# Weight splits, dealt gate tiles and the order of the query and key splits in the second attention of a two-block transformer kernel

## The reference

```python
FOX_HEADS = 16
FOX_HEAD_DIM = 64
FOX_SCALE = 1.0 / math.sqrt(FOX_HEAD_DIM)

    proj = u @ w_in[l]
    (cq, ckv, k_pe_raw, z_mla, fq, fk, fv, f_logit, z_fox, gate_a, gate_b) = jnp.split(proj, split_idx, axis=-1)
    ...
    log_f = jax.nn.log_sigmoid((f_logit + fox_forget_b[l]).astype(jnp.float32)).transpose(0, 2, 1)
    cum = jnp.cumsum(log_f, axis=-1)
    o_fox = causal_block_attention(fox_heads(fq), fox_heads(fk), fox_heads(fv), FOX_SCALE, cum)
    o_fox = o_fox.transpose(0, 2, 1, 3).reshape(B, L, FOX_WIDTH)
    y_fox = (o_fox * jax.nn.silu(z_fox)) @ w_br_fox[l]
```

## Time and profile before

| | |
|---|---|
| median of 3 runs | 1583.72 us |
| the runs | 1583.72, 1578.91, 1584.73 us |
| the profiled execution | 1581.14 us |
| its span in the trace | 1579.3 us |
| mean granted TensorE clock | 0.995 of full speed |
| PE busy | 1535.2 us (97%) |
| DVE busy | 837.9 us (53%) |
| ACT busy | 694.3 us (44%) |

### The profile page before, as it was taken

One profiled execution on the slowest core, in us unless ns is written; L12 is line 12 of the kernel. 1 busy time (PEld: TensorE's weight loads), 2 busy tenths in 40 slices (PEclk: granted clock), 3 DMA queues, 4 the chain that ended last, 5 costly groups with the idle time before them and its releaser, 6 DMA issues.

```text
span 1579.3 us, 24007 instructions
## 1 busy us (share of the span) xinstructions
PE 1535.2 (97%) x10287; PEld 1349.9 (85%) x10287; DVE 837.9 (53%) x1234; ACT 694.3 (44%) x1036; POOL 3.6 (0%) x16
## 2 busy tenths in 40 slices
PE   7999999999999999999999899999999999999998
PEld 7999999999999988997888677778899787778888
DVE  6467766644655565653344576643223565543343
ACT  6555666654343222222333655633222766643232
POOL 0000000000000000000000000000000000000000
PEclk9999999999999999999999999999999999999999
DMA  6212112113332232322224100122322111122322
GB/s 228 81 58 84 54 54 72 51 41 135 107 106 82 81 107 81 107 81 97 96 76 125 30 28 1 54 81 85 102 81 81 54 54 54 54 67 81 107 81 81
DMA packets 130541, 125.46 MB, mean 79 GB/s; under 512 B 20169, under 2 KB 128484, under 8 KB 130052
## 3 DMA queue, kind: packets, MB, share of 16 engines
q1 hardware_dynamic: 129956, 120.36, 24.1%
q0 software_dynamic: 464, 3.56, 0.6%
q10 hardware_dynamic: 16, 0.00, 0.0%
HBM read 119.66 MB, written 4.26 MB: 78 GB/s over the span
## 4 chain that ended last, share of the span: by engine, by line
PE 86%; DVE 7%; ACT 4%; issue 3%; DMA 0%; DVEq 0%; SPq 0%; ACTq 0%
PE PS L841 73%; PE PS L953 3%; PE PS L1167 2%; DVE wlo L1786 2%; PE PS L1110 2%; PE PS L1132 2%; DVE small L2303 1%; ACT Pm L1296 1%; ACT xka L1296 1%; ACT whi L1296 0%; PE PS L1115 0%; PE PS L1144 0%; PE PS L1116 0%; PE PS L965 0%; PE PS L1001 0%
## 5 line engine op out<-in xcount | busy, mean ns | idle before, releaser
L841 PE MATMUL PS<-zhi,whi 128*128 128x258 f32 (+2 forms) x1872 | 487.0, 320 | 8.1 <-DVE zlo L1832 3.4
L841 PE MATMUL PS<-zlo,whi 128*128 128x258 f32 (+2 forms) x1872 | 475.4, 314 | 0.0
L841 PE MATMUL PS<-zhi,wlo 128*128 128x258 f32 (+2 forms) x1872 | 474.9, 314 | 0.0
L841 PEld LDWEIGHTS PS<-zhi,whi 128*128 128x128 f32 x1872 | 309.1, 190 | 33.3 <-issue 8.3
L841 PEld LDWEIGHTS PS<-zhi,wlo 128*128 128x128 f32 x1872 | 307.6, 189 | 21.5
L841 PEld LDWEIGHTS PS<-zlo,whi 128*128 128x128 f32 x1872 | 307.9, 189 | 18.8
L1786 DVE TENSOR_TENSOR wlo<-raw,whi 128x2048 fp32r<-128x2048 f32 (+2 forms) x114 | 247.7, 2173 | 123.2 <-ACT whi L1296 122.9
L1296 ACT ACTIVATE whi<-raw 128x2048 fp32r<-128x2048 f32 (+2 forms) x114 | 207.3, 1819 | 155.3 <-DMA raw<-in_w_up 55.9
L1296 ACT ACTIVATE Pm<-PS,small 128x144 f32<-128x144 f32 (+3 forms) x128 | 68.7, 540 | 79.1 <-DVE small L2303 79.1
L2303 DVE TENSOR_REDUCE small<-PS 128x1 f32<-128x144 f32 (+3 forms) x128 | 62.5, 502 | 37.5 <-PE PS L1117 36.8
L841 PE MATMUL PS<-ghi,whi 128*128 128x512 f32 x176 | 69.7, 396 | 2.2 <-DVE glo L2198 2.2
(11 more groups left out here) (351 smaller groups left out, 2157.6 us busy)
## 6 DMA issues: line engine op xcount, KB each, us to landing
raw<-in_w_in SPq DMA_DIRECT2D x50, 1024.0 KB, 5.2
raw<-in_w_up SPq DMA_DIRECT2D x22, 1024.0 KB, 5.1
raw<-in_w_out SPq DMA_DIRECT2D x8, 1024.0 KB, 5.3
raw<-in_w_down SPq DMA_DIRECT2D x8, 1024.0 KB, 5.1
raw<-in_w_br_mla SPq DMA_DIRECT2D x4, 1024.0 KB, 5.4
raw<-in_w_br_fox SPq DMA_DIRECT2D x4, 1024.0 KB, 5.3
raw<-in_w_down SPq DMA_DIRECT2D x4, 768.0 KB, 4.6
hspill<-hT SPq DMA_DIRECT2D x1, 2112.0 KB, 8.7
```

The lines of the kernel that those rows point to most:

```text
L841: ins = mm(o_, l_, r_, start=first, stop=last)
```

## The change

Three edits, all in the second attention.

1. DVE takes the low parts of a weight unit in the same pass in which ACT takes the high part. It no longer stands at the start of pass h+1; it stands at the second block of pass h, behind the reciprocal sums and ahead of the product `omla` and of `split_lo(h+1)` (the new argument `ahead`).
2. The tiles ("xz", 0) and ("xz", 1) are dealt over the passes 13, 14 and 15 in single steps (`XZ_STEPS`); the pass 16 keeps ("xz", 2).
3. ACT makes both copies of the query ahead of both copies of the key. DVE waits for the query's two copies, makes `xqa` and `xqb`, and only then waits for the key's and makes `xkb`. In pass 0 the query is split before the key's tile is taken out of its accumulator.

```diff
+            XZ_STEPS = {(13, 0): ((0, 0),), (13, 1): ((0, 1),), (13, 2): ((0, 2),), (13, 3): ((0, 3),),
+                        (13, 4): ((0, 4), (0, 5)), (14, 0): ((0, 6),), (14, 1): ((0, 7),), (14, 2): ((1, 0),),
...
             def fox_fill(h, i):
+                for x, k in XZ_STEPS.get((h, i), ()):
+                    if k == 0:
+                        portion[0] = gemm_steps(("xz", x))
+                    ins = portion[0](k)
+                    if k == KT - 1:
+                        ins.then_inc(pe_mark, 1)
                 x = h // 2 + 1 + h % 2
                 if x < KT:
                     name = (("xk", "xq")[h % 2], x)
-                elif h - 14 in (0, 1, 2):
-                    name = ("xz", h - 14)
+                elif h == HEADS:
+                    name = ("xz", 2)
...
-                tile_freed(act, ("xk", h // 2))
                 q = fq[h // 2 % 2]
                 A_(xqa[i][r, :], q[r, :], ACT.Copy).then_inc(fox_hi, 1)
+                A_(xqb[i][r, :], q[r, :], ACT.Copy).then_inc(fox_hi, 1)
+                if h == 0:
+                    fk_out(0)
+                tile_freed(act, ("xk", h // 2))
                 A_(xka[i][r, :], fk[r, :], ACT.Copy).then_inc(fox_hi, 1)
-                A_(xqb[i][r, :], q[r, :], ACT.Copy).then_inc(fox_hi, 1)
                 A_(xka[i][o, :], fk[r, :], ACT.Copy).then_inc(fox_hi, 1)
...
-            def attention(A, project, between):
+            def attention(A, project, between, ahead):
...
+                            ahead(h)
                             if h >= 3 and h % 2 == 1:
...
-                dve.wait_ge(fox_hi, 4 * (h + 1))
+                dve.wait_ge(fox_hi, 4 * h + 2)
                 q = fq[h // 2 % 2]
                 V.tensor_tensor(xqa[i][o, :], q[r, :], xqa[i][r, :].bitcast(F32), ALU.subtract).then_inc(fox_lo, 1)
+                V.tensor_copy(xqb[i][o, :], pick[o, h:h + 1].bitcast(F32).broadcast_to([64, SEQ])).then_inc(fox_lo, 1)
+                dve.wait_ge(fox_hi, 4 * h + 4)
                 V.tensor_tensor(xkb[i][r, :], fk[r, :], xka[i][r, :].bitcast(F32), ALU.subtract).then_inc(fox_lo, 1)
-                V.tensor_copy(xqb[i][o, :], pick[o, h:h + 1].bitcast(F32).broadcast_to([64, SEQ])).then_inc(fox_lo, 1)
...
-                w_low(*XU_AT.get(h - 1, ()))
-
-            attention(fox, fox_project, lambda h: split_lo(h + 1) if h < HEADS - 1 else None)
+
+            attention(fox, fox_project, lambda h: split_lo(h + 1) if h < HEADS - 1 else None,
+                      lambda h: w_low(*XU_AT.get(h, ())))
```

More of the change, by code:

```diff
@@ L1728, in fox_project @@
                     act.wait_ge(xv_turned, KT)
-                    fk_out(0)
                     split_hi(0)
@@ L2392, in q_out @@
                                                  in1=trig[:, 0, NM:T], op0=ALU.mult, op1=ALU.mult), n)
-            attention(mla, mla_project, lambda h: None)
+            attention(mla, mla_project, lambda h: None, lambda h: None)
             def gated(kind, A, b):
```

## The result

The changed kernel took 1570.89 us in the median of five runs (1570.11 to 1574.25), the kernel before, beside it, 1581.0 (1578.91 to 1584.73). The ratio is 0.9934, with a 95% interval of 0.9919 to 0.995: 10.1 us less between the medians, 10.4 by the ratio. Run again twice later it gave 0.9924 (0.991 to 0.9938) and 0.9936 (0.9923 to 0.9949). The forecast was 1575.3 with a range from 1571 to 1581.

A forecast was written before the change was run, and what follows sets the result against it. TensorE, busy 97% of the span, was taken to bound the kernel. Terms 1.1 + 1.5 + 0.5 + 1.0 + 3.4 + 1.6 - 0.3 - 0.4 = 8.4 us, off the median 1583.72, gave 1575.3 us, range 1571 to 1581.

The forecast's parts named there:

- the ceiling of this change: Second attention: at most TensorE's 8.8 us of idle time and 1.6 us of slow clock can be won, 10.4 us.
- My terms without clock and groups: Second attention: gains from removed waits, less pass 14's 0.4; left out are clock (1.6) and five more step groups (0.3 lost).
- The estimate of 0.16 us for a break: Dealt gate tiles: by the Trainium skill's formulas each break in TensorE's stream costs 0.16 us, 0.8 us for five.
- passes 4, 8, 12: 0.5 us: Passes 4, 8, 12: maxima of blocks 0 and 1 no longer stand behind the low part; 0.5 us gained.
- Query ahead of key: Passes 0 and 1: DVE starts its splits after two ACT copies, not four; the whole wait goes, 1.1 us.
- Low parts: Moved into DVE's idle time a pass earlier: 1.5 us in passes 2, 6, 10; 0.5 in 4, 8, 12; 1.0 in 1.
- Tiles: Pass 13: dealt gate steps fill all waits, 3.4 us, and save 1.6 of clock; groups cost 0.3, pass 14 waits 0.4.
- Waits that only move on: Rival, passes 1, 4, 8, 12, 14: part of the waits moves on; gain 6.4 us, 1577.3; 23 in 100.
- The clock falls anyway: Rival, thin passes 13 to 15: the clock falls once, 1.6 us come back; gain 6.8, 1576.9; 10 in 100.
- The change does little: Rival: key copies end last, or pass 13's waits reappear in 14 and 15; gain 3.4 or less, 1580.5; 5 in 100.
- The slower case: Rival: low part not covered in eight passes, 18 us added, less 8.4: 10 us slower, 1594; 5 in 100.

The follow-up runs named there:

- e5: The changed kernel with ten stalls of TensorE added on purpose in the five gate tiles behind the attention: 1578.05 us, ratio 0.9966.
- e1: The kernel before with only the third edit, query copies ahead of key copies on ACT and DVE waiting for two, then four: 1575.47 us, ratio 0.9962.
- e2: The kernel before with only the first edit, low parts of the weights taken in the odd pass itself: 1578.46 us, ratio 0.9983.
- e7: The changed kernel with TensorE's first turn ahead of the filling tile in passes 1, 2, 4, 6, 8, 10 and 12: 1569.85 us, ratio 0.9921.
- e9: The changed kernel with TensorE's first turn ahead of the filling tile only in the even passes 2 to 12: 1567.92 us, ratio 0.991.
- e4: The kernel before with the first and third edits, without the dealt tiles: 1575.96 us, ratio 0.9966.
- e3: The kernel before with only the second edit, gate steps dealt six to pass 13 and five each to 14 and 15: 1577.85 us, ratio 0.9979.
- e6: The changed kernel with an unused DVE reduction of some 2.2 us ahead of each low part in the eight odd passes: 1579.47 us, ratio 0.9988.

## Why the prediction was off, point by point

**What bounds the kernel: right, but the ceiling was not one.** TensorE's idle time and its slow clock were what could be won. The sentence "the ceiling of this change is 8.8 + 1.6 = 10.4 us" is wrong: the price of 16 stalls was not in it. With 0.25 each it would have been 14.

**The idle time that goes: right.** My terms without clock and groups, 1.1 + 1.5 + 0.5 + 1.0 + 3.4 - 0.4, make 7.1. In the traces it went from 8.8 in 16 stalls to 1.7 in nine, 7.1. TensorE is busy 7.1 us more of the 210, where I expected some 8.

**The step that failed: each stall was costed at its idle figure.** Seven stalls fewer, at the 0.25 of e5, are 1.75 us that stand in no term. Idle time 7.1, stalls 1.75, clock 1.7 and groups -0.3 make 10.25, against 10.2 measured. Only the sum comes out so well. On top of the idle time, passes 0 and 1 gave 0.55 for one stall fewer, passes 4, 8 and 12 0.2 each, and in pass 13 three stalls fewer and five groups more gave 0.2 together; no run measures the groups alone. The estimate of 0.16 us for a break, which the prediction sets against the dealing, was applied to no stall; e5 measured 0.16 to 0.17 of lost overlap at each. The missing price shows most where stalls are short: "passes 4, 8, 12: 0.5 us" was 1.2. In those the wait itself was right (0.19 each) and its price 0.4 each. e1 and e2 each give that same 0.4 in those passes by different means, and e7 and e9 give 0.39 for each stall of 0.16.

**The second step that failed: the anchor.** I took the sum of one profiled execution off the median of three runs, 1583.72, though that execution itself stood at 1581.14. The five runs beside the changed kernel have a median of 1581.0, the later ones 1581.13 (20), 1581.53 (20) and 1581.74 (9). From 1581.14 the same 8.4 us give 1572.7, inside the range. This was worth 2.6 us, the stalls 1.8. The lower end of the range, 1571, was the ceiling of 10.4 us taken off 1581, so a gain of 10.2 from 1581 ends beside it. With medians of 1569.15, 1570.89 and 1571.33 for the changed kernel it is chance on which side of it one of them falls.

**Query ahead of key: right in mechanism and size** for passes 0 and 1 (2.1 forecast, 2.4 measured). e1 shows it as the strongest of the three alone. DVE's `xqa` waits for ACT's second copy in eight passes; in the others it follows the low part.

**Low parts: right.** 1.5 forecast and 1.6 measured in passes 2, 6 and 10. In pass 1, of which I said that most of the wait goes, 0.36 of 1.21 is left, for two reasons. The turn itself came 2.3 us earlier, as reckoned, but TensorE was there 1.5 earlier and not 1.1. And DVE's splits start at 1242.7, behind the low part and not behind the query copies; in e1, where no low part stands there, this wait is gone. In the odd passes nothing moved, as reckoned.

**Tiles: right, small terms as well.** Pass 14 waits 0.19 (0.4 forecast). The 0.45 of the earlier trace rows stood at the second scores of pass 14 (128x272), not at its first, and went as well. The clock stays at 1.00, worth 1.7: behind pass 13 it fell in all four traces without the dealt tiles (before, e1, e2, e4) and in none of the eight with them. What I did not see is that this term rests on the other two: without them the tiles give 2.8.

**The rivals.** Waits that only move on: not here; but e3 is that rival, with two edits left out. The clock falls anyway: in the attention it did not, in any of the changed kernel's three traces. The change does little: no, pass 13 gave its term and nothing came back in 14 or 15. The slower case is real as a mechanism and far off: 2.2 us more in front of each low part cost 8.0 us, and even then the kernel is no slower than before.

## What to carry to other kernels

On an engine whose rows overlap, count the stalls as well as their idle time: here each costs 0.2 to 0.25 us on top of its figure, so six waits of 0.16 us, 1.0 us by their figures, were worth 2.4. When a filler is spread over more passes, check the chain of the other engines in the passes that get less of it; the edit that shortens that chain has to come first. Anchor a sum on the execution it was read from, and treat the median of three runs as another draw of the same scatter.

## What was not expected of the hardware

Whether the clock falls behind a given wait differs between executions, and so does the length of the slow stretch. Behind the same 2.2 us wait near 725 us it fell in six of twelve traces. In passes 13 and 14, 3.4 us of idle time came with 1.7 us of clock lost in the kernel before, 2.1 us of it with 1.7 in e1, 3.25 and 2.4 with 3.4 in e2 and e4, while the 1.9 us of e3 cost nothing. In e6 a single wait of 2.56 us was enough:

```profile
1245.00:1250.00 5.00, 5.00 (x25) 4.38 (x23) 1.80 (x8) 2.74 (x9) 0.00 (x0) 0.66 0.00 0
```

The slow stretch lasted some 3.4 us in the kernel before and some 6.8 us in e2, both at 0.50 of the full clock, 1.2 GHz. The Trainium skill, "TensorE: Matmul & The Clock Gate", in its part on the clock gate, says that the point at which the clock rises varies by half a microsecond from run to run. These two lengths differ by more.
